# The first norm of a two-layer kernel: its weights spread over two banks by matmul, its high and low parts taken from the turned bank, the first token tile fed through alone, and identity matmuls between

## The chip, the cores and the metric

The kernel runs on one core of a Trainium2 chip. The metric is the device time of one execution in microseconds (us), as the median of several runs. The engines are TensorE (PE; its weight loads are listed as PEld), VectorE (DVE), ScalarE (ACT), GpSimd (POOL), and SyncE (SP), which issues most DMAs. A q behind an engine's name is its queue of DMA issues.

## The reference, cut to what matters

Two transformer-like layers run one after the other on 512 tokens of width 1024, in f32. The change touches only the first lines of the first layer:

```python
def rmsnorm(x, g):
    xf = x.astype(jnp.float32)
    y = xf * lax.rsqrt(jnp.mean(xf * xf, axis=-1, keepdims=True) + EPS)
    return (y * g.astype(jnp.float32)).astype(x.dtype)
...
        u = rmsnorm(h, norm_mix_pre)
        proj = u @ w_in
```

`proj` is then cut into the inputs of a short convolution and of a sparse attention; an output product, a cross attention over a memory, and a gated feed-forward stage follow. The second layer has its own norms, an mLSTM, a neighbourhood attention, a memory attention and a feed-forward stage. Every large product is a product with a weight matrix of 1024 or more rows.

## The kernel before

**Tiling.** The 512 tokens are four token tiles of 128 (`ST` = 4), each with 1024 features: `h[:, j, :]`. A product needs features on the partitions, so each normed token tile is turned: eight transposes of 128x128, four into each of two PSUM banks (`TB`, banks 4 and 5), whose result goes to `xT_high` and `xT_low`. Each f32 number is split into a high part, rounded to the format that TensorE takes at one column a beat (`fp32r`), and a low part, the rest. A product is then three matmuls: high by high, low by high and high by low. Weights are split in the same way: a chunk of 128x2048 lands in `raw`, ACT casts it to `w_high` (line 950, in `high`), and POOL subtracts to get `w_low` (line 805, in `low_parts`), in four pieces of 512.

**Order.** Each engine's program is written out by hand, and semaphores tie the engines together. `Own.link` and `Own.tell` make an engine wait for its own last instruction. The weight chunks are loaded by SP in a fixed order into three `raw` slots; a slot is loaded again when both parts of its old chunk have been made. `w_high` and `w_low` have two slots each.

**The head of the program.** For each token tile j of the first norm (phase `"x"`): ACT takes the mean square of row sums (`stat`, lines 958 and 959); DVE takes the reciprocal and multiplies the rows (`xn`, lines 1480 and 1490) into one of two `stage` buffers; PE turns them (`turn`, line 2181); DVE multiplies the turned bank by the norm weights, which lie one to a partition in `gcol`, into `qbuf` (`ql`, line 1516); ACT casts `qbuf` to `xT_high` (`hi`, line 973); DVE subtracts to `xT_low` (`ql`, line 1523). Phases in `DIRECT` have no step through `qbuf`: ACT casts straight from the turned bank (line 970), and DVE subtracts from the bank too (`lows`, line 1499).

The weights `norm_mix_pre` get into `gcol` by a load of 8 rows of 128 into `rows_in`, a transpose into bank 7 (line 2342) and a DVE copy (line 1539). The other vectors come the same way later (`vectors`, line 2348).

PE's own order is: the turned weights, token tiles 0 and 1 turned, the first chunk's product for token features of tile 0, tile 2 turned, product 1, tile 3 turned, product 2, the small vectors, product 3, then four products with the second chunk. A product here is 4 pairs of matmuls with `w_high` (lines 2291 and 2292) and 4 with `w_low` (line 2295), each 128x512. `SB` are banks 6 and 7, `ident` is the 128x128 identity, `ones` a 128x128 tile of ones, both written by POOL at the start. POOL's order at the start is its constants, `w_low` of chunks 0 and 1, then 32 one-column memsets of `invf` (line 812), which the rotary angles need.

## Time and profile before

| | us |
|---|---|
| median of 3 runs | 1724.48 (1724.47 to 1725.52) |
| the profiled execution's own time | 1727.71 |
| its span in the profile | 1726.0 |
| PE busy | 1662.4 (96%) |
| POOL / ACT / DVE busy | 729.8 / 663.8 / 621.0 |

The span runs from the first to the last instruction of the profiled execution, which took 1.7 us more than its span and 3.2 us more than the median of the runs. PE is busy nearly all the time. The mean granted clock is 0.987 of the full 2.4 GHz.

### The profile page before, as it was taken

To read this page: it belongs to the slowest core of one execution; us is meant where nothing else is said; L and a number is where in the kernel's file an instruction comes from. 1 tells how busy PE (TensorE), PEld (TensorE's weight loads), DVE (VectorE), ACT (ScalarE), POOL (GpSimd) and SP (SyncE) were. 2 spreads that over 40 slices of the span, in tenths; PEclk is the share of its full clock that TensorE was granted. 3 is DMA by queue.
4 is the path that set the end of the run, shared out by engine and by line. 5 is a ranking of instruction groups with operands and counts; after the bars stand their busy time and mean duration, and the time that the engine had idled before them with its cause. 6 is when DMAs were issued, how large, how long until landed. Compare 5 with 4: busy or idle time off the path is not lost. (4 is left out here: it accounts for less than half of the span.)

```text
span 1726.0 us, 22688 instructions
## 1 busy us (share of the span) xinstructions
PE 1662.4 (96%) x8699; PEld 1326.5 (77%) x8699; DVE 621.0 (36%) x1165; ACT 663.8 (38%) x1009; POOL 729.8 (42%) x639
## 2 busy tenths in 40 slices
PE   7989889999899999999988999999999999999999
PEld 5767667777678888878877787767788888888887
DVE  6432765442333101101137544454555331212131
ACT  5223567453343233222234534343554441313140
POOL 5223324462143444453434544323354354544443
PEclk9999999999999999999999999999999999999999
DMA  5243201332032332343221334222254323232321
GB/s 176 76 147 82 74 26 51 123 131 90 25 98 74 122 98 73 98 146 98 86 87 51 98 100 147 78 74 84 74 202 152 98 80 100 90 98 98 98 98 49
DMA packets 153020, 166.07 MB, mean 96 GB/s; under 512 B 11997, under 2 KB 114512, under 8 KB 152912
## 3 DMA queue, kind: packets, MB, share of 16 engines
q1 hardware_dynamic: 145296, 151.22, 27.7%
q10 hardware_dynamic: 7616, 13.41, 2.2%
q8 instruction: 69, 1.13, 0.3%
q14 instruction: 39, 0.32, 0.1%
HBM read 155.69 MB, written 9.30 MB: 96 GB/s over the span
## 5 line engine op out<-in xcount | busy, mean ns | idle before, releaser
L805 POOL TENSOR_TENSOR w_low<-raw,w_high 128x512 fp32r<-128x512 f32 x501 | 662.0, 1352 | 877.0 <-ACT w_high L950 876.6
L950 ACT CAST w_high<-raw 128x2048 fp32r<-128x2048 f32 x127 | 239.3, 1884 | 244.1 <-PE bank L2295 230.7
L2300 PE MATMUL bank<-xT_high,w_high 128*128 128x512 f32 (+1 forms) x672 | 249.7, 377 | 0.0
L2301 PE MATMUL bank<-xT_low,w_high 128*128 128x512 f32 (+1 forms) x672 | 248.9, 375 | 0.0
L2291 PE MATMUL bank<-w_high,hid_high 128*128 128x512 f32 x432 | 171.9, 398 | 0.0
L2292 PE MATMUL bank<-w_high,hid_low 128*128 128x512 f32 x432 | 171.7, 398 | 0.0
L2304 PE MATMUL bank<-xT_high,w_low 128*128 128x512 f32 (+1 forms) x672 | 156.7, 375 | 1.8 <-POOL w_low L805 1.7
L2205 PE MATMUL bank<-xT_high,w_high 128*128 128x512 f32 (+1 forms) x360 | 152.3, 423 | 0.7 <-ACT qbuf L1317 0.4
L2300 PEld LDWEIGHTS bank<-xT_high,w_high 128*128 128x128 f32 x672 | 127.8, 190 | 22.4
L2301 PEld LDWEIGHTS bank<-xT_low,w_high 128*128 128x128 f32 x672 | 127.7, 190 | 22.4
L2207 PE MATMUL bank<-xT_high,w_low 128*128 128x512 f32 (+1 forms) x360 | 142.4, 396 | 0.0
L2206 PE MATMUL bank<-xT_low,w_high 128*128 128x512 f32 (+1 forms) x360 | 142.0, 394 | 0.0
L2304 PEld LDWEIGHTS bank<-xT_high,w_low 128*128 128x128 f32 x672 | 120.6, 188 | 24.9 <-POOL w_low L805 2.6
L2295 PE MATMUL bank<-w_low,hid_high 128*128 128x512 f32 x432 | 119.6, 397 | 0.0
L2291 PE MATMUL bank<-w_high,xT_high 128*128 128x512 f32 x256 | 102.6, 401 | 3.3 <-DVE xT_low L1523 3.2
L2292 PE MATMUL bank<-w_high,xT_low 128*128 128x512 f32 x256 | 100.8, 394 | 0.0
L2295 PEld LDWEIGHTS bank<-w_low,hid_high 128*128 128x128 f32 x432 | 81.7, 189 | 20.0 <-POOL w_low L805 0.2
L2291 PEld LDWEIGHTS bank<-w_high,hid_high 128*128 128x128 f32 x432 | 81.7, 189 | 19.8
L2292 PEld LDWEIGHTS bank<-w_high,hid_low 128*128 128x128 f32 x432 | 81.7, 189 | 19.8
L2157 DVE TENSOR_TENSOR h<-h,bank 128x512 f32<-128x512 f32 x40 | 27.5, 688 | 173.6 <-PE bank L2295 173.5
L2205 PEld LDWEIGHTS bank<-xT_high,w_high 128*128 128x128 f32 (+1 forms) x360 | 67.8, 188 | 24.5 <-issue 9.0
L1861 DVE TENSOR_TENSOR qbuf<-silu,bank 128x512 f32<-128x512 f32 x22 | 15.1, 688 | 187.7 <-PE bank L2304 187.7
(427 smaller groups left out, 2533.1 us busy)
## 6 DMA issues: line engine op xcount, KB each, us to landing
raw<-in_w_in SPq DMA_DIRECT2D x33, 1024.0 KB, 5.2
raw<-in_w_down SPq DMA_DIRECT2D x26, 1024.0 KB, 5.0
raw<-in_w_gate_up SPq DMA_DIRECT2D x44, 512.0 KB, 5.0
raw<-in_w_up SPq DMA_DIRECT2D x16, 1024.0 KB, 5.3
raw<-in_w_kv_x SPq DMA_DIRECT2D x8, 1024.0 KB, 5.3
raw<-in_w_out SPq DMA_DIRECT2D x8, 1024.0 KB, 5.1
gate_dram<-qbuf ACTq DMA_DIRECT2D x20, 256.0 KB, 2.0
sg<-gate_dram ACTq DMA_DIRECT2D x6, 768.0 KB, 5.4
```

The costliest lines, as they stand in the source:

```text
L805: ins = pool.tensor_tensor(low[:, cs], full[:, cs], high[:, cs], ALU.subtract)
L950: own.tell(act.copy(split_slot(c, wh), split_slot(c, raw)), wh_done)
L2157: own.tell(dve.tensor_tensor(y, y, src[:, :], ALU.add), dense_v)
L2205: pe.matmul(ps, ah, bh, start=first, stop=False)
L2206: pe.matmul(ps, ah, bl, start=False, stop=False)
L2207: return pe.matmul(ps, al, bh, start=False, stop=last)
L2291: pe.matmul(ps[:, :], xh[:, k, js], ch[:, q, :], start=first and q == 0, stop=False)
L2292: pe.matmul(ps[:, :], xl[:, k, js], ch[:, q, :], start=False, stop=False)
L2295: mm = pe.matmul(ps[:, :], xh[:, k, js], cl[:, q, :], start=False, stop=last and q == len(ks) - 1)
L2300: pe.matmul(ps[:, t0:t1], ch[:, k, cs], xh[:, k, t0:t1], start=q == 0, stop=False)
L2301: pe.matmul(ps[:, t0:t1], ch[:, k, cs], xl[:, k, t0:t1], start=False, stop=False)
L2304: mm = pe.matmul(ps[:, t0:t1], cl[:, k, cs], xh[:, k, t0:t1], start=False, stop=q == len(ks) - 1)
```

## The change

1. The norm weights come as one row of 1024 (`mix_row`, on one partition), and two matmuls with a row of ones copy them onto all 128 partitions, one half into bank 6 and one into bank 7.
2. For phase `"x"`, `xn` is now two `scalar_tensor_tensor` of 128x512: rows by reciprocal by the weights in the bank. `"x"` joins `DIRECT`: highs and lows come from the turned bank, with no `qbuf`.
3. The order on ACT, DVE and PE lets token tile 0 through alone: its highs before tile 1's statistics, its lows before tile 1's `xn`, its product before tile 1 is turned. Tile 1 is turned in the middle of product 0, between its matmuls with `w_high` and those with `w_low`. ACT's cast of the second chunk (`high(1)`) moves behind the statistics of tile 3.
4. PE gets 15 matmuls of `ident` by `ident` into bank 3, whose result nobody reads: 2 ahead of the spreading, 5 behind it, 8 behind the turning of tile 0.
5. POOL writes `ones` ahead of `ident`, and the 32 memsets of `invf` ahead of `w_low`; chunk 1's `w_low` comes after `zT` and `pc`.
6. The column table loses five vectors (40 of 100 rows), of which four were loaded by SP and not read from it; SP issues four DMAs less.

```diff
--- before.py
+++ after.py
@@ -43,8 +43,7 @@
 ATT_ORDER = (0, 3, 1, 2)
 
 
-VECS = [("norm_mix_pre", 8), ("norm_x_pre", 8), ("norm_mem", 8), ("norm_ffn_pre", 8), ("g_mix_2", 8),
-        ("g_mem_2", 8), ("g_ffn_2", 8), ("norm_conv_out", 4), ("norm_attn_out", 4),
+VECS = [("norm_mem", 8), ("g_mem_2", 8), ("norm_conv_out", 4), ("norm_attn_out", 4),
         ("conv_w", 12), ("conv_w_2", 20), ("conv_b_2", 4)]
 COL = {}
 _n = 0
@@ -58,7 +57,7 @@
 GAIN_LOADS = sum(P // d for _, d in HEAD_GAINS)
 HOMES = {"gu0": 0, "if": 0, "up0": 1, "vx": 2}
 NATURAL = ("hx", "hf", "h2", "h4")
-DIRECT = NATURAL + ("hm", "hna")
+DIRECT = NATURAL + ("x", "hm", "hna")
 
 
 class Chunk:
@@ -255,11 +254,11 @@
 
     out, base, scaled = [], 0, 0
     for phase, ntok, banks, kt0, gain in (
-            ("x", ST, 2, 0, COL["norm_mix_pre"]), ("mem", MT, 2, 0, COL["norm_mem"]),
-            ("att", ST, 1, 4, COL["norm_attn_out"]), ("hx", ST, 2, 0, COL["norm_x_pre"]),
-            ("hf", ST, 2, 0, COL["norm_ffn_pre"]), ("mem2", MT, 2, 0, COL["g_mem_2"]),
-            ("h2", ST, 2, 0, COL["g_mix_2"]), ("hm", ST, 1, 0, None),
-            ("hna", ST, 1, 4, None), ("h4", ST, 2, 0, COL["g_ffn_2"])):
+            ("x", ST, 2, 0, None), ("mem", MT, 2, 0, COL["norm_mem"]),
+            ("att", ST, 1, 4, COL["norm_attn_out"]), ("hx", ST, 2, 0, None),
+            ("hf", ST, 2, 0, None), ("mem2", MT, 2, 0, COL["g_mem_2"]),
+            ("h2", ST, 2, 0, None), ("hm", ST, 1, 0, None),
+            ("hna", ST, 1, 4, None), ("h4", ST, 2, 0, None)):
         for j in ATT_ORDER if phase == "att" else range(ntok):
             out.append((phase, j, banks, base, kt0, gain, scaled))
             base += banks
@@ -364,6 +363,7 @@
         posi = at("posi", o + 13728, [P, 5], I32)
         invf = at("invf", o + 13760, [P, 32])
         ang = at("ang", 24640, [P, 5, 32])
+        mix_row = at("mix_row", 53312, [1, D])
         angk = at("angk", 25280, [P, 5, 32])
         rows_in = at("rows_in", 25920, [NCOL, P])
         pe_in = at("pe_in", 26560, [CMP, 2, 2, HD])
@@ -601,7 +601,7 @@
                 sp.dma_start(h[:, j, :], xv[:, j, :]).then_inc(x_in[j], 16)
 
             def vector_loads():
-                for name, n in VECS[1:]:
+                for name, n in VECS:
                     src = a[name]
                     src = src.rearrange("(r q) -> r q", q=P) if len(src.shape) == 1 else \
                         src.rearrange("k (r q) -> (k r) q", q=P)
@@ -766,10 +766,10 @@
             own.link(pool.memset(posi[:, :], 0))
             own.link(pool.memset(small[:, :], 0.0))
             own.tell(pool.memset(eps_col[:, :], EPS), const_ready)
+            own.link(pool.memset(ones[:, :], 1.0))
             own.link(pool.memset(ident[:, :], 0.0))
             own.tell(pool.affine_select(out=ident[:, :], in_=ident[:, :], compare_op=ALU.not_equal, fill=1.0,
                                         base=0, pattern=[[-1, P]], channel_multiplier=1), const_ready)
-            own.link(pool.memset(ones[:, :], 1.0))
             own.link(pool.memset(causal[:, :], 0.0))
             own.link(pool.affine_select(out=causal[:, 384:512], in_=causal[:, 384:512], compare_op=ALU.is_ge,
                                         fill=NEG, base=0, pattern=[[-1, P]], channel_multiplier=1))
@@ -807,9 +807,9 @@
                             own.mark(ins, wl_done)
                     own.tell(ins, wl_done)
 
-            low_parts(1)
             for j in range(32):
                 own.link(pool.memset(invf[:, j:j + 1], float(np.float32(THETA ** (-j / 32.0)))))
+            low_parts(0)
             own.link(pool.memset(zT[:, :, 0:2], 0.0))
             own.tell(pool.memset(pc[:, :, :, :], 0.0), const_ready)
             low_parts(G["gates"].chunks[-1].n)
@@ -981,15 +981,6 @@
                 dst, src = parts[-1]
                 own.tell(act.copy(dst, src), hi_done)
 
...
             def evac(group, write, between=None):
 
                 g = G[group]
@@ -1003,7 +994,7 @@
                         between(c)
 
 
-            act.dma_start(rows_in[0:8, :], a["norm_mix_pre"].rearrange("(r q) -> r q", q=P)).then_inc(mix_in, 16)
+            act.dma_start(mix_row[:, :], a["norm_mix_pre"].rearrange("(o d) -> o d", o=1)).then_inc(mix_in, 16)
             for i, n in enumerate(("pe_kc", "pe_vc")):
                 for g in range(2):
                     act.dma_start(pe_in[:, i, g, :], a[n]).then_inc(rows_in_s, 16)
@@ -1011,12 +1002,12 @@
             own.link(act.activation(rms[:, 63:64], eps_col[:, 0:1], ACT.Sqrt))
             stat(("x", 0), h[:, 0, :], D)
             high(0)
+            hi(ntile["x", 0])
             stat(("x", 1), h[:, 1, :], D)
-            hi(ntile["x", 0])
             stat(("x", 2), h[:, 2, :], D)
-            high(1)
             hi(ntile["x", 1])
             stat(("x", 3), h[:, 3, :], D)
+            high(1)
             hi(ntile["x", 2])
             hi(ntile["x", 3])
 
@@ -1480,6 +1471,14 @@
                 own.link(dve.reciprocal(rms[:, k:k + 1], rms[:, k:k + 1]))
                 if i >= 2:
                     dve.wait_ge(tr_done, NT[i - 2][3] + NT[i - 2][2])
+                if phase == "x":
+                    dve.wait_ge(vec_tr, 1)
+                    for b in range(2):
+                        cs = slice(S * b, S * b + S)
+                        ins = dve.scalar_tensor_tensor(out=stage[:, i % 2, cs], in0=h[:, j, cs], scalar=rms[:, k:k + 1],
+                                                       in1=SB[b][:, :], op0=ALU.mult, op1=ALU.mult)
+                        own.tell(ins, xn_ready) if b else own.link(ins)
+                    return
                 if phase in NATURAL:
                     dve.wait_ge(gnat_in, 16 * (NATURAL.index(phase) + 1))
                     own.tell(dve.scalar_tensor_tensor(out=stage[:, i % 2, :], in0=h[:, j, :], scalar=rms[:, k:k + 1],
@@ -1522,25 +1521,22 @@
                     q = qbuf[:, r % 2, 0:n * P].rearrange("p (k t) -> p k t", k=n)
                     own.tell(dve.tensor_tensor(dst, q, top.bitcast(F32), ALU.subtract), lo_done)
 
-            def norm(phase, ntok, width):
-                for j in range(ntok):
-                    xn(phase, j, width)
-                    if j:
-                        ql(phase, j - 1)
-                ql(phase, ntok - 1)
-
             def tile_in(name, t):
                 n = G[name].tiles[t]
                 dve.wait_ge(dense_done, n + 1)
                 return tile_bank(n)
 
 
-            dve.wait_ge(vec_tr, 1)
-            own.link(dve.tensor_copy(gcol[:, 0:8], SB[1][:, 0:8]))
-
-            norm("x", ST, D)
+            xn("x", 0, D)
+            lows("x", 0)
+            xn("x", 1, D)
+            xn("x", 2, D)
+            lows("x", 1)
+            xn("x", 3, D)
+            lows("x", 2)
+            lows("x", 3)
             dve.wait_ge(vec_tr, 2)
-            own.link(dve.tensor_copy(gcol[:, 8:NCOL], SB[0][:, 8:NCOL]))
+            own.link(dve.tensor_copy(gcol[:, 0:NCOL], SB[0][:, 0:NCOL]))
             own.link(dve.tensor_copy(peT[:, :, :], SB[0][:, P:P + 2 * CMP].rearrange("p (i c) -> p i c", i=2)))
 
             dve.wait_ge(const_ready, 4)
@@ -2255,7 +2251,7 @@
                     low_seen[0] = need
                     pe.wait_ge(wl_done, need)
 
-            def product(c, k_tile, xh, xl, ntok=S, piece=None, part=None):
+            def product(c, k_tile, xh, xl, ntok=S, piece=None, part=None, between=None):
 
                 if True:
                     g = c.group
@@ -2290,6 +2286,8 @@
                             for q, k in enumerate(ks):
                                 pe.matmul(ps[:, :], xh[:, k, js], ch[:, q, :], start=first and q == 0, stop=False)
                                 pe.matmul(ps[:, :], xl[:, k, js], ch[:, q, :], start=False, stop=False)
+                            if between:
+                                between()
                             for q, k in enumerate(ks):
                                 low_ready(c, q)
                                 mm = pe.matmul(ps[:, :], xh[:, k, js], cl[:, q, :], start=False,
@@ -2337,14 +2335,22 @@
                 turned_ready(phase, ST if phase not in ("mem", "mem2") else MT)
 
 
+            def keep_warm(n):
+                for _ in range(n):
+                    pe.matmul(bank[3][:, 0:P], ident[:, :], ident[:, :], start=True, stop=True)
+
             pe.wait_ge(const_ready, 2)
+            keep_warm(2)
             pe.wait_ge(mix_in, 16)
-            pe.transpose(SB[1][:, 0:8], rows_in[0:8, :], ident[0:8, 0:8]).then_inc(vec_tr, 1)
+            for b in range(2):
+                mm = pe.matmul(SB[b][:, :], ones[0:1, :], mix_row[:, S * b:S * b + S], start=True, stop=True)
+            mm.then_inc(vec_tr, 1)
+            keep_warm(5)
             turn("x", 0)
-            turn("x", 1)
+            keep_warm(8)
 
             def vectors():
-                pe.wait_ge(rows_in_s, 16 * (len(VECS) - 1 + 2 * GROUPS))
+                pe.wait_ge(rows_in_s, 16 * (len(VECS) + 2 * GROUPS))
                 pe.transpose(SB[0][:, 0:NCOL], rows_in[:, :], ident[0:NCOL, 0:NCOL])
                 for i in range(2):
                     mm = pe.transpose(SB[0][:, P + CMP * i:P + CMP * (i + 1)], pe_in[:, i, :, :].rearrange(
@@ -2353,7 +2359,7 @@
             q_first, q_last = G["q"].chunks
             for j in range(ST):
                 turned_ready("x", j + 1)
-                product(q_first, j, xTh, xTl)
+                product(q_first, j, xTh, xTl, between=(lambda: turn("x", 1)) if j == 0 else None)
                 if j < 2:
                     turn("x", j + 2)
                 if j == 2:
```

On PE, from its first matmul to the end of product 0, the kernel before has (`stage` are the normed rows, `rows_in` the 8 rows of norm weights):

```order
L2342 MATMUL bank<-ident,rows_in 128x8
L2181 MATMUL bank<-ident,stage 128x128 x16
L2291 MATMUL bank<-w_high,xT_high 128x512
L2292 MATMUL bank<-w_high,xT_low 128x512
...
L2291 MATMUL bank<-w_high,xT_high 128x512
L2292 MATMUL bank<-w_high,xT_low 128x512
L2295 MATMUL bank<-w_low,xT_high 128x512 x4
```

and with the change, over the same place:

```order
L2340 MATMUL bank<-ident 128x128 x2
L2346 MATMUL bank<-mix_row,ones 128x512 x2
L2340 MATMUL bank<-ident 128x128 x5
L2177 MATMUL bank<-ident,stage 128x128 x8
L2340 MATMUL bank<-ident 128x128 x8
L2287 MATMUL bank<-w_high,xT_high 128x512
...
L2288 MATMUL bank<-w_high,xT_low 128x512
L2177 MATMUL bank<-ident,stage 128x128 x8
L2293 MATMUL bank<-w_low,xT_high 128x512 x4
L2177 MATMUL bank<-ident,stage 128x128 x8
L2287 MATMUL bank<-w_high,xT_high 128x512
```

The second half of the 16 transposes has moved from ahead of product 0 to inside it.

On ACT, from the cast of the first weight chunk to the last highs of the norm, the kernel before has:

```order
L950 CAST w_high<-raw 128x2048
L958 ACTIVATE junk,rms<-h 128x1024
L959 ACTIVATE rms<-rms,eps_col 128x1
L973 CAST xT_high<-qbuf 128x4x128 x2
L958 ACTIVATE junk,rms<-h 128x1024
L959 ACTIVATE rms<-rms,eps_col 128x1
L950 CAST w_high<-raw 128x2048
L973 CAST xT_high<-qbuf 128x4x128 x2
L958 ACTIVATE junk,rms<-h 128x1024
L959 ACTIVATE rms<-rms,eps_col 128x1
L973 CAST xT_high<-qbuf 128x4x128 x4
```

and with the change:

```order
L950 CAST w_high<-raw 128x2048
L970 CAST xT_high<-bank 128x4x128 x2
L958 ACTIVATE junk,rms<-h 128x1024
L959 ACTIVATE rms<-rms,eps_col 128x1
L958 ACTIVATE junk,rms<-h 128x1024
L959 ACTIVATE rms<-rms,eps_col 128x1
L970 CAST xT_high<-bank 128x4x128 x2
L958 ACTIVATE junk,rms<-h 128x1024
L959 ACTIVATE rms<-rms,eps_col 128x1
L950 CAST w_high<-raw 128x2048
L970 CAST xT_high<-bank 128x4x128 x4
```

Tile 0's highs moved ahead of tile 1's statistics, and the second cast of weights moved back by one tile's statistics and one tile's highs.

On DVE, over the first two token tiles, the kernel before has:

```order
L1480 RECIPROCAL rms<-rms 128x1
L1490 TENSOR_SCALAR stage<-h,rms 128x1024
L1480 RECIPROCAL rms<-rms 128x1
L1490 TENSOR_SCALAR stage<-h,rms 128x1024
L1516 TENSOR_TENSOR qbuf<-bank,gcol 128x512 x2
L1523 TENSOR_TENSOR xT_low<-qbuf,xT_high 128x4x128 x2
```

and with the change:

```order
L1471 RECIPROCAL rms<-rms 128x1
L1478 SCALAR_TENSOR_TENSOR stage<-h,rms,bank 128x512 x2
L1498 TENSOR_TENSOR xT_low<-bank,xT_high 128x4x128 x2
L1471 RECIPROCAL rms<-rms 128x1
L1478 SCALAR_TENSOR_TENSOR stage<-h,rms,bank 128x512 x2
L1471 RECIPROCAL rms<-rms 128x1
L1478 SCALAR_TENSOR_TENSOR stage<-h,rms,bank 128x512 x2
L1498 TENSOR_TENSOR xT_low<-bank,xT_high 128x4x128 x2
```

Tile 0's lows no longer stand behind tile 1's rows, and the two multiplications into `qbuf` are gone.

## Rows read from the trace of the kernel before

**Rows 1.** The page: busy time of PE, and the chain that ended last by engine.

```profile
PE 1662.4 (96%) x8699; PEld 1326.5 (77%) x8699; DVE 621.0 (36%) x1165; ACT 663.8 (38%) x1009; POOL 729.8 (42%) x639
...
PE 32%; DVE 0%; issue 0%; ACT 0%; DVEq 0%; ACTq 0%
```

**Rows 2.** Timeline of PE: start, length in us, instruction, [idle before, its releaser].

```profile
2.92 0.24 PE L2342 MATMUL bank<-ident,rows_in 8*128 8x8 f32 x1 [2.92 <-DMA rows_in<-in_norm_mix_pre]
7.51 1.97 PE L2181 MATMUL bank<-ident,stage 128*128 128x128 f32 x8 [4.35 <-DVE stage L1490]
...
15.94 0.79 PE L2291 MATMUL bank<-w_high,xT_high 128*128 128x512 f32 x1 [0.88 <-DVE xT_low L1523]
...
21.23 1.26 PE L2181 MATMUL bank<-ident,stage 128*128 128x128 f32 x8
22.24 0.48 PE L2291 MATMUL bank<-w_high,xT_high 128*128 128x512 f32 x1
...
25.08 1.04 PE L2181 MATMUL bank<-ident,stage 128*128 128x128 f32 x8
...
32.39 0.39 PE L2291 MATMUL bank<-w_high,xT_high 128*128 128x512 f32 x1
```

**Rows 3.** Timeline of ACT, same columns.

```profile
4.92 1.06 ACT L958 ACTIVATE junk<-h 128x1024 bf16<-128x1024 f32 x1
...
6.10 0.30 ACT L959 ACTIVATE rms<-rms,eps_col 128x1 f32<-128x1 f32 x1
7.17 1.90 ACT L950 CAST w_high<-raw 128x2048 fp32r<-128x2048 f32 x1 [0.77 <-DMA raw<-in_w_in]
...
34.82 1.91 ACT L950 CAST w_high<-raw 128x2048 fp32r<-128x2048 f32 x1
```

**Rows 4.** Timeline of DVE, same columns.

```profile
6.50 0.16 DVE L1480 RECIPROCAL rms<-rms 128x1 f32<-128x1 f32 x1 [3.14 <-ACT rms L959]
6.70 0.75 DVE L1490 TENSOR_SCALAR stage<-h,rms 128x1024 f32<-128x1024 f32 x1
...
12.28 1.42 DVE L1516 TENSOR_TENSOR qbuf<-bank,gcol 128x512 f32<-128x512 f32 x2
13.79 2.10 DVE L1523 TENSOR_TENSOR xT_low<-qbuf,xT_high 128x512 fp32r<-128x512 f32 x2
```

**Rows 5.** Timeline of POOL, same columns.

```profile
4.58 0.14 POOL L783 MEMSET rpb_zero<- 1x64 f32 x1
9.22 5.39 POOL L805 TENSOR_TENSOR w_low<-raw,w_high 128x512 fp32r<-128x512 f32 x4 [4.50 <-ACT w_high L950]
17.99 6.36 POOL L805 TENSOR_TENSOR w_low<-raw,w_high 128x512 fp32r<-128x512 f32 x4 [3.38 <-ACT w_high L950]
24.41 4.94 POOL L812 MEMSET invf<- 128x1 f32 x32
```

**Rows 6.** Groups by form: line, engine, operation, shapes, count | busy us, mean ns | idle before.

```profile
L2053 DVE SCALAR_TENSOR_TENSOR decay<-bank,decay 128x512 f32<-128x512 f32 x8 | 5.5, 692 | 10.4 <-PE bank L2659 10.3
L1499 DVE TENSOR_TENSOR xT_low<-bank,xT_high 128x512 fp32r<-128x512 f32 x32 | 22.1, 692 | 15.5 <-ACT xT_high L970 14.5
L970 ACT CAST xT_high<-bank 128x512 fp32r<-128x512 f32 x32 | 18.8, 587 | 21.4 <-PE bank L2181 20.8
```

**Rows 7.** Timeline around a later norm whose highs come from the bank.

```profile
359.73 1.03 PE L2181 MATMUL bank<-ident,stage 128*128 128x128 f32 x8
360.42 1.20 ACT L970 CAST xT_high<-bank 128x512 fp32r<-128x512 f32 x2 [0.66 <-PE bank L2181]
```

**Rows 8.** Timeline of PE where plain f32 columns run at the full clock.

```profile
228.80 1.12 PE L2493 MATMUL bank<-conv_scale,ones 128*128 128x512 f32 x2 [0.74 <-DVE conv_scale L1671]
229.86 1.13 PE L2450 MATMUL bank<-kT,qT 64*128 64x512 f32 x4
```

**Rows 9.** Timeline of PE around a later rise of the clock.

```profile
109.32 0.79 PE L2205 MATMUL bank<-xT_high,w_high 128*128 128x512 f32 x1
...
114.03 0.40 PE L2207 MATMUL bank<-xT_high,w_low 128*128 128x512 f32 x1
```

More of the change, by code:

```diff
@@ L982, in hi_grid @@
                 own.tell(act.copy(dst, src), hi_done)
-            def norm(phase, ntok, width):
-                for j in range(ntok):
-                    src = SOURCES[phase]
-                    stat((phase, j), src[:, j, :], width)
-                    if j:
-                        hi(ntile[phase, j - 1])
-                hi(ntile[phase, ntok - 1])
             def evac(group, write, between=None):
@@ L1523, in ql @@
                     own.tell(dve.tensor_tensor(dst, q, top.bitcast(F32), ALU.subtract), lo_done)
-            def norm(phase, ntok, width):
-                for j in range(ntok):
-                    xn(phase, j, width)
-                    if j:
-                        ql(phase, j - 1)
-                ql(phase, ntok - 1)
             def tile_in(name, t):
```

## The prediction

> **What bounds the kernel now.** I read the page first. PE is busy 96% of the span, and the chain that ended last has PE with 32%, and 0% each for DVE, ACT and their queues [rows 1]: once its products run, PE waits for almost nobody. So what moves PE's first products moves the end by as much, provided that no stage further on was paced by something that the change leaves where it was. Hence I read the timeline of PE over the head of the program, then those of the engines it waits for.
>
> PE's first product starts at 15.94, and the first of the four products with the second chunk at 32.39 [rows 2]. From there on the order is as before. The quantity that I follow is that second start.
>
> Two things are lost before it. First, a relay: the rows of tile 0 are ready at 7.45 [rows 4] and turned from 7.51 to 9.48 [rows 2], but DVE takes them up only at 12.28, because tile 1's rows stand ahead of them; then come four steps through `qbuf`. Second, the clock. Product 0 takes 21.23 - 15.94 = 5.29 us, product 1 only 25.08 - 22.24 = 2.84 [rows 2], for the same 12 matmuls. The turning takes 1.97 us at 7.51 and 1.04 at 25.08. So PE runs at 1.2 GHz up to about 21.2 and at 2.4 GHz from there. It had worked without a pause since 15.94, so the rise came 5.3 us after steady work began. At the later rise, steady products begin at 109.32 and the short duration is there at 114.03 [rows 9]: 4.7 us.
>
> **The change, step by step.** Times are those of the profiled execution.
>
> *Weights spread.* POOL writes `ones` ahead of `ident`, which makes `ident` about 0.35 us later, at 2.4; the two first identity matmuls run in the wait for the load. The load of 8 rows of 512 bytes is there by 2.92 [rows 2]. The new one moves the same 4 KB to one partition; the trace has no such load. Bounds: 2.92, and 4.92, by when the 512 KB of tile 0 are there [rows 3]. I take 2.95. The two spreading matmuls have 512 plain f32 columns; the nearest row starts two of them 1.06 us ahead of the next group at 2.4 GHz [rows 8], so at most 2.1 us for two at 1.2 GHz. The weights are then in the banks at 5.1 (at the late bound 7.1). DVE can't use them before tile 0's reciprocal ends at 6.66 [rows 4]. So the step costs nothing at 2.95, and 0.4 us at the late bound. The gain column's copy on DVE was idle time anyway.
>
> *Five identity matmuls.* A 128-column pass cost 0.24 us at 1.2 GHz (1.97 for 8) [rows 2], so they end at 6.3; PE would be idle until 8.2. Cost nothing.
>
> *Tile 0's rows.* One `tensor_scalar` of 0.75 us [rows 4] becomes two `scalar_tensor_tensor` of 128x512 with one input in a bank. The same operation with such an input takes 0.692 [rows 6], so 6.70 + 2 x 0.73 = 8.13: 0.7 us later than before. PE turns from 8.18 to 10.15.
>
> *Highs and lows.* In the later norm, ACT starts the highs 0.69 us after the turning starts at the full clock [rows 7]; at half the clock the first four transposes take 1 us and the step about 0.2. So ACT starts at 9.35, when its cast of the first chunk is done (9.07) [rows 3]. Two highs of 0.587 and two lows of 0.692 [rows 6] interleave: highs 9.35 to 9.95 and 10.25 to 10.85, lows to 10.6 and 11.6. The eight identity matmuls fill PE from 10.15 to 12.0, and since they are in order ahead of the product they, not the lows, set its start: **product 0 starts at 12.0** instead of 15.94.
>
> *The clock.* PE now works steadily from 8.18. By the two cases above the rise comes 4.7 to 5.3 us later, at 12.9 to 13.5; I take 13.4. Eight matmuls with `w_high` from 12.0: 3.3 of them at 0.427 us, the rest at 0.23, to 14.5 (512 columns at 1.2 GHz are 0.427 us; 0.23 is a twelfth of a product at the full clock, rounded down).
>
> *Tile 1.* ACT takes its statistics only after tile 0's highs: 10.87 + 1.48 (4.92 to 6.40 for tile 0) [rows 3] = 12.35; DVE has the rows at 14.08. PE turns them from 14.5; highs to 16.4, lows at 16.55 and 17.25. Meanwhile PE does the four matmuls with `w_low`. POOL has to do 32 memsets first (4.94 us, now from 4.75 to 9.7), then four pieces of 5.39/4 = 1.35 [rows 5]: ready at 11.1, 12.4, 13.8 and 15.1, and wanted from 15.5 on. Cost nothing; with the slower pace of 6.36 for four, the last comes at 16.1, just when it is wanted.
>
> *Tiles 2 and 3.* Turning 2 needs the banks free, at 16.55 and 17.25, so product 1 runs from 17.8 to 20.55. ACT does tile 3's statistics (to 17.9) and now the second weight cast (to 19.8) ahead of tile 2's highs: these come at 19.8 and 20.45, lows at 21.2 and 21.9. PE waits for them 0.7 us and once more 0.2; product 2 from 22.45 to 25.2, small vectors 0.4, product 3 from 25.6 to **28.35**, where it was 32.39. The gain at this point is **4.0 us**.
>
> *Behind it.* `w_low` of the second chunk is made from 19.85 to at most 26.2 (6.36) [rows 5] and wanted at 30.2. The rotary angles hang on the small vectors, which come 4 us sooner; the third chunk's cast, at 34.82 [rows 3], waits for the sine behind them and moves along. The four loads that SP no longer issues were behind the data that PE waits for; worth nothing. With no other engine in the chain [rows 1] I let all 4.0 us through. The profile gives 1726.0 - 4.0; the profiled run took 1727.71, 3.2 more than the median, so the sum goes to the median: 1724.48 - 4.0 = **1720.5**.
>
> A bound on each side. If the rise comes before 12.0, the products with `w_high` end at 13.8, but tile 1's rows are there only at 14.08, so the gain is at most 4.4 (1720.1). If it comes at 15.0, they end at 15.25 and all behind is 0.75 later: gain 3.3 (1721.2).
>
> **What a rule would make of it.** The group of two plain f32 matmuls of 512 columns and the group behind it start 1.06 us apart [rows 8], 0.53 each; one beat a column is 0.213, so this is two passes and a start. The Trainium skill (FP8 and Floating Point Precision, TensorE Precision Notes) says that true FP32 takes four passes through the array. By it the eight identity matmuls at 1.2 GHz would take 3.4 us instead of 1.9, which is its own case below; the trace disagrees with it.
>
> **The rivals.**
> - *The identity matmuls don't bring the clock up.* They multiply mostly zeros, and the turning at 7.51 was not followed by a rise before 21.2. Then steady work counts from 12.0, and the rise comes near 17: product 0 with `w_high` to 15.4, turning 1 to 17.4, lows of tile 1 at 18.45, product 1 from 19.0, product 2 from 23.7, second chunk at 29.5. Gain 2.85: 1721.6. Nothing in the trace decides; chance 0.17.
> - *Identity matmuls twice as long* (four passes): product 0 starts at 13.6, gain about 2.5: 1722.0. Against it stands the row on plain f32; chance 0.03.
> - *Something further on holds its time*, so that the later stages give part of the 4 us back. For it: PE has 1726.0 - 1662.4 = 63.6 us of idle time in all [rows 1], of which not 12 lie ahead of product 0. Against it: those waits are on ACT, DVE and POOL, which themselves wait for PE. Half given back: 1722.5; chance 0.07.
> - *Slower: the row of weights comes late.* It is one run of 4 KB where there were eight of 512 bytes, and may queue behind the row tiles and weight chunks that are loaded at the same time. Each us by which the banks are ready after 6.66 moves tile 0's rows. If the load comes with the first weight chunk, at 7.17 [rows 3], the banks are ready at 9.3 and the gain is 1.4 (1723.1): chance 0.04. From a landing at 8.6 on, the change is slower; behind the fourth row tile and the second chunk, at about 12, it would be 1727.9: chance 0.04. Against both: the 8-row load was through in 2 us under the same traffic.
> - *More than counted*: the later stretches at half the clock fall differently on the work, and the run is nearer 1718.5. They can fall worse as well, which is in the forecast's own range. Chance 0.07.
>
> **The numbers.** The forecast has 0.58. 0.2% of this time is 3.4 us, about what a measurement of this kernel can tell from no change, so the border lies at 1721.0. The forecast's own range is 1719.6 to 1721.6, mostly below the border: four fifths of 0.58 are faster, with the last rival 0.54; the rest of the forecast and the cases at 1721.6 to 1723.1 make 0.41 "within"; slower 0.05. The range that leaves out the slower case and the outer part of the last rival is 1718.4 to 1723.2.
>
> **What would show each step.** In the profile after: the spreading matmuls by 3 and the banks ready by 5.2; tile 0's rows at 8.1; the first product at about 12.0, its matmuls turning from 0.43 to 0.23 us apart at 12.9 to 13.5; tile 1 turned at 14.5; the second chunk's first product at about 28.35 and the third cast near 30.7. The prediction is wrong if the first product starts after 12.5 (late weights or long identity matmuls), if the pace rises after 15, or if the second chunk starts at 28.4 and the end has moved less: then a later stage holds its own time.

## The result, and the profile after

| | before | after |
|---|---|---|
| median of 4 runs each, same chip, us | 1725.0 (1724.47 to 1729.08) | 1711.77 (1705.77 to 1716.15) |
| profiled execution, us | 1727.71 | 1716.15 |
| its span, us | 1726.0 | 1714.4 |
| mean granted clock | 0.987 | 0.985 |

The ratio of the times is 0.9922 [0.9905, 0.9940]: 13.2 us less, where I had forecast 4.0, and outside the range. The page of the kernel after has PE as busy as before; 33 more PE records, and less busy time than in [rows 1]:

```profile
PE 1660.4 (97%) x8732; PEld 1330.9 (78%) x8732; DVE 616.3 (36%) x1160; ACT 663.6 (39%) x1009; POOL 728.8 (43%) x639
...
PE 32%; DVE 0%; issue 0%; ACT 0%; DVEq 0%; ACTq 0%
```

The timeline of PE over the head, which answers to [rows 2]:

```profile
2.40 1.22 PE L2340 MATMUL bank<-ident 128*128 128x128 f32 x4 [2.40 <-POOL ident L771]
3.55 3.78 PE L2346 MATMUL bank<-mix_row,ones 1*128 1x512 f32 x4
7.25 2.50 PE L2340 MATMUL bank<-ident 128*128 128x128 f32 x10
9.55 1.92 PE L2177 MATMUL bank<-ident,stage 128*128 128x128 f32 x8
11.26 2.88 PE L2340 MATMUL bank<-ident 128*128 128x128 f32 x16
13.89 0.48 PE L2287 MATMUL bank<-w_high,xT_high 128*128 128x512 f32 x1
...
15.82 1.04 PE L2177 MATMUL bank<-ident,stage 128*128 128x128 f32 x8
16.61 1.17 PE L2293 MATMUL bank<-w_low,xT_high 128*128 128x512 f32 x4
18.12 1.29 PE L2177 MATMUL bank<-ident,stage 128*128 128x128 f32 x8 [0.34 <-DVE xT_low L1498]
...
29.98 0.39 PE L2287 MATMUL bank<-w_high,xT_high 128*128 128x512 f32 x1
```

Two things stand in it. The counts: two identity matmuls in the code are four records here, five are ten, eight are sixteen, and the two spreading matmuls are four. A plain f32 matmul thus shows as two records, a transpose of f32 as one (x8 for eight). And the second chunk's product starts at 29.98, where it was 32.39: the head has given 2.4 us, not 4.0. The timelines of DVE and ACT, against [rows 4] and [rows 3], show the first delay, the rows of tile 0 waiting for the weights in the bank:

```profile
7.45 1.53 DVE L1478 SCALAR_TENSOR_TENSOR stage<-h,rms,bank 128x512 f32<-128x512 f32 x2 [0.78 <-PE bank L2346]
11.39 0.69 DVE L1498 TENSOR_TENSOR xT_low<-bank,xT_high 128x512 fp32r<-128x512 f32 x1 [2.41 <-ACT xT_high L970]
```

```profile
10.70 0.58 ACT L970 CAST xT_high<-bank 128x512 fp32r<-128x512 f32 x1 [1.52 <-PE bank L2177]
...
32.37 1.91 ACT L950 CAST w_high<-raw 128x2048 fp32r<-128x2048 f32 x1
```

The span is 11.6 us shorter, so more than 9 us come from behind 30 us, where the code of the engines is as before. I set each PE instruction of after against the same one of before. How much earlier it starts:

| at (us) | 100 | 300 | 500 | 700 | 900 | 1240 | 1400 | 1500 | 1600 | end |
|---|---|---|---|---|---|---|---|---|---|---|
| earlier by (us) | 2.4 | 5.1 | 5.7 | 6.8 | 8.2 | 6.8 | 7.4 | 8.4 | 9.7 | 11.5 |

(The steps back, of 1.4 us between 900 and 1240 and of 1.5 us behind 1240, are two stretches of 3.4 us at half the clock that only after has.) Of the 2.7 us between 100 and 300, 1.6 are the products behind 137.65, which ran at half the clock in before and at the full clock in after, and 0.9 one turning at 221.46 for the same reason; the other differences there nearly cancel. Behind 300 the lead grows in no single wait. It grows steadily while PE runs the products that read `hid`, `yT`, `hmT` or `oxT`, and stays flat in those that read `xT`. The timeline of PE in such a product, of before and then of after, both at a granted clock of 1.00; between the first and the last row of each lie five products of 12 matmuls:

```profile
630.12 1.10 PE L2295 MATMUL bank<-w_low,hid_high 128*128 128x512 f32 x4
...
632.93 1.10 PE L2295 MATMUL bank<-w_low,hid_high 128*128 128x512 f32 x4
...
644.18 1.10 PE L2295 MATMUL bank<-w_low,hid_high 128*128 128x512 f32 x4
```

```profile
632.14 1.08 PE L2293 MATMUL bank<-w_low,hid_high 128*128 128x512 f32 x4
...
634.89 1.07 PE L2293 MATMUL bank<-w_low,hid_high 128*128 128x512 f32 x4
...
645.87 1.07 PE L2293 MATMUL bank<-w_low,hid_high 128*128 128x512 f32 x4
```

The sixty matmuls took 644.18 - 630.12 = 14.06 us before, 234 ns each, and 645.87 - 632.14 = 13.73 us after, 229 ns each. The same instructions with the same operands run 2% faster. There are 1296 such matmuls on `hid` (at 5.4 ns that makes 7.0 us), 192 each on `yT` and `hmT`, 192 on `oxT`.

What differs is where the operands lie. `hid`, `yT`, `hmT`, `oxT` and `memT` are views into one block, `arena` (`at(...)`). It is allocated behind `gcol`, the column table, which shrank by 40 of its 100 f32 a partition: the arena starts at byte 147776 of a partition after, and at 147936 before. Modulo 256 that is 64 after and 224 before. `xT`, `w_high` and `w_low` lie ahead of it and begin at 128 modulo 256 in both.

### The profile page after: what moved, and what is told of

Its sections match the earlier page's. It is cut to its first block and busy times, and to the rows that moved or that the text cites. A ratio compares the mean times of both kernels' runs of the same rounds, so it can differ in the third digit from the quotient of the medians.

```text
span 1714.4 us, 22737 instructions
## 1 busy us (share of the span) xinstructions
PE 1660.4 (97%) x8732; PEld 1330.9 (78%) x8732; DVE 616.3 (36%) x1160; ACT 663.6 (39%) x1009; POOL 728.8 (43%) x639
## 5 line engine op out<-in xcount | busy, mean ns | idle before, releaser
L2288 PEld LDWEIGHTS bank<-w_high,hid_low 128*128 128x128 f32 x432 | 81.6, 189 | 17.2
```

The costliest lines, as they stand in the source:

```text
L2288: pe.matmul(ps[:, :], xl[:, k, js], ch[:, q, :], start=False, stop=False)
```

## The experiments

Theory P (placement): the 9 us come from the position of the arena alone. Rival H (head): they are a late result of the earlier start, of loads or of clock stretches. The second question is what the identity matmuls, the spreading and the new order each do in the head.

All runs in one table. The change is the median less that of the kernel before on the same chip (1725.2 for e1 to e4, 1724.2 for e5 to e8, 1725.18 for e9 to e12). "2nd chunk" is the start of its first product in the profiled execution. "Pace" is worked out from the trace: for each pair of operands, the mean time from one PE start to the next of the 512-column matmuls at the full clock, times their number, summed over all pairs; before has 1248.2 us.

| run | change, us | ratio | 2nd chunk | pace, us |
|---|---|---|---|---|
| before | | | 32.39 | 1248.2 |
| after | -13.2 | 0.9922 [0.9905, 0.9940] | 29.98 | 1238.8 |
| e1_pad32 | -5.3 | 0.9972 [0.9962, 0.9981] | 32.66 | 1245.1 |
| e2_pad96 | -9.3 | 0.9943 [0.9929, 0.9956] | 32.50 | 1238.8 |
| e3_after_pad32 | -4.8 | 0.9969 [0.9956, 0.9981] | 29.57 | 1246.8 |
| e4_no_ident | -13.8 | 0.9919 [0.9906, 0.9933] | 29.09 | 1238.8 |
| e5_hid64 | -7.2 | 0.9955 [0.9938, 0.9972] | 32.38 | 1240.3 |
| e6_noid_pad64 | -11.9 | 0.9929 [0.9915, 0.9944] | 30.11 | 1237.6 |
| e7_noid_pad128 | -3.8 | 0.9978 [0.9969, 0.9986] | 29.75 | 1246.3 |
| e8_old_order | -13.2 | 0.9922 [0.9907, 0.9938] | 29.42 | 1238.6 |
| e9_front64 | -13.2 | 0.9920 [0.9907, 0.9933] | 30.08 | 1238.7 |
| e10_all_at_128 | -16.1 | 0.9904 [0.9891, 0.9916] | 29.93 | 1235.1 |
| e11_ident_turned | -16.4 | 0.9900 [0.9887, 0.9914] | 28.77 | 1238.9 |
| e12_order_only | +2.4 | 1.0011 [1.0002, 1.0020] | 33.70 | 1248.5 |

### Placement without the change: e1, e2

The kernel before, with an unused tensor right ahead of the arena, in e1 of 8 f32 a partition (arena at 0 modulo 256), in e2 of 24 (at 64, as in after):

```diff
+        sb("pad", [P, 8])       # e1; e2: sb("pad", [P, 24])
         arena_bytes = 77888
```

> The kernel before with one unused tile of 32 bytes a partition ahead of the arena, so that everything in the arena (hid, yT, hmT, oxT, memT) lies 32 bytes further on, at a multiple of 64 bytes; nothing else is changed. Theory A, the place of the arena: 512-column matmuls that stream from the arena were 234 ns apart before and 229 with the change, those that stream xT, ahead of the arena, 227 in both; here they fall to about 229, some 1900 matmuls by 5 ns, so 9 us less than before: about 1716. Theory B, the time behind the head is won by the head's order (other half-clock stretches, other meetings of engines): no change, 1725, and the pace stays 234.

> The kernel before with an unused tile of 96 bytes, so that the arena's start is 64 more than a multiple of 128, as it is in the changed kernel. Theory A with steps of 64 bytes: as with 32 bytes, about 1716. Theory A with steps of 128 bytes: one of the two padded kernels gains 9 us and the other not, or less. Theory B: 1725.

With the old head whole (second chunk at 32.50), e2 is 9.3 us faster, and its pace is that of after to 0.1 us. Theory P holds, and rival H falls: an unused tensor brings what the change brought behind the head. e1, at another position, has a third of it in its pace (3.1 us) and is 5.3 us faster, between the 9 us and the nothing that I had expected of the two theories. (The expectations speak of matmuls that stream from the arena. In the products of 512 columns only `hmT` is the moving operand, the one that is streamed; `hid`, `yT` and `oxT` are the stationary one.)

### The change with the gain taken away: e3, e7

The kernel after with 8 f32 ahead of the arena (at 96), and, without identity matmuls, with 32 f32 (at 192):

```diff
+        sb("pad", [P, 8])       # e3; e7: sb("pad", [P, 32]), and no keep_warm
         arena_bytes = 77888
```

> The changed kernel with an unused tile of 32 bytes ahead of the arena, so that the arena starts 32 more than a multiple of 64, as in the kernel before. Theory A: the pace in the arena is 234 ns again, and only the head's 2.4 us are left: about 1722.5. Theory B: as the changed kernel, 1712.

> As the last, with 128 bytes ahead of the arena: again 64 more than a multiple of 128. If steps of 128 bytes decide, as without the tile: pace 229, 1711.4.

Both keep the early head and lose most of the rest: -4.8 and -3.8 us. That is the order of what the head alone is worth. For e7 I had expected the pace of after, if steps of 128 bytes decide; they don't.

### Which position, and relative to what: e5, e6, e9, e10

e5 is e1 with the two `hid` tensors alone put at 64; e6 is e4 with the arena at 128; e9 is e4 with 16 f32 ahead of `h`, which moves every tensor behind it, weights and arena alike, by 64 bytes; e10 is e4 with the `hid`, `hmT` and `oxT` highs shifted by 64 within the arena, so that they and their lows lie at 128.

```diff
-        hidh, hidl = at("hid_high", 0, [P, 8, S], F32R), at("hid_low", 16384, [P, 8, S], F32R)
+        hidh, hidl = at("hid_high", 64, [P, 8, S], F32R), at("hid_low", 16448, [P, 8, S], F32R)   # e5, e10
+        sb("pad", [P, 16])      # e6, ahead of the arena
+        sb("front", [P, 16])    # e9, ahead of h
```

> The kernel before with the 32-byte tile (arena at a multiple of 128 bytes), and of the arena's tensors only hid_high and hid_low moved another 64 bytes, into a gap behind them. Theory A, the pace hangs on the bytes at which the operand itself lies: in the down projections the 232.6 ns of the 32-byte kernel become about 229, as at 64 more than a multiple of 128, some 1290 matmuls by 3.5 ns, so 4.5 us less than with the 32-byte tile (1719.9 there), about 1715.5, and the hmT and yT matmuls keep that kernel's pace. Rival C, it is the arena as a whole (its other tensors, which ScalarE, VectorE and GpSimd read and write meanwhile): the pace stays 232.6 and the time 1720.

> The changed kernel without identity matmuls (1711.4), with 64 bytes ahead of the arena: a multiple of 128, and the same bytes modulo 256 as the tensors ahead of the arena, which are streamed at 227. If being at the same place modulo 256 as those is what counts, the pace falls to 227 and the time to about 1709. If it is as with the 32-byte tile on the kernel before, also at a multiple of 128 but not at the same place modulo 256, the pace is 232.5 and the time 1715.

> The changed kernel without identity matmuls, with an unused tile of 64 bytes ahead of the very first tile, h: every tensor lies 64 bytes further on, and none moves against another. If it is the distance between the two operands of a matmul that counts (modulo 256 the arena lies 64 under the weights), nothing changes: 1711.4, xT 227 and hid 229. If it is each operand's own place modulo 256, with 128 the best: the arena is now at 128 and hid goes to 227, but xT and the weights go to 192, where hid had 231 to 236: some 3600 matmuls by 4 to 8 ns, 15 to 28 us slower: 1726 to 1740.

> The changed kernel without identity matmuls, with hid_high and hid_low, hmT_high and oxT_high moved 64 bytes within the arena, so that they too lie at 128 modulo 256, as yT, hmT_low and oxT_low already do. By the table of paces so far: hid from 229.1 to 227, some 1290 matmuls by 2.1 ns, and a little for the others: 3 us less than 1711.4, so 1708.4. If the tensors' other users count, no change.

The mean ns from start to start, worked out from the traces. The first of a pair is the moving operand, the second the stationary one:

| pair | before | after | e1 | e3 | e5 | e6 | e7 | e9 | e10 |
|---|---|---|---|---|---|---|---|---|---|
| arena begins at, mod 256 | 224 | 64 | 0 | 96 | 0 | 128 | 192 | 128 | 64 |
| w_high, hid_high | 234.4 | 229.2 | 232.7 | 232.3 | 229.1 | 226.9 | 235.7 | 229.1 | 226.9 |
| w_high, hid_low | 234.3 | 229.5 | 232.4 | 234.5 | 229.6 | 226.8 | 231.2 | 229.6 | 226.7 |
| w_low, hid_high | 234.2 | 228.4 | 232.6 | 233.4 | 228.4 | 227.0 | 233.4 | 228.4 | 226.9 |
| w_high, yT_low | 233.2 | 226.9 | 228.6 | 234.7 | 228.5 | 235.7 | 232.0 | 227.0 | 226.8 |
| hmT_high, w_high | 234.3 | 227.4 | 237.2 | 232.4 | 237.6 | 233.2 | 231.2 | 227.3 | 226.9 |
| xT_low, w_high | 227.5 | 227.5 | 227.6 | 227.5 | 227.4 | 227.6 | 227.6 | 227.5 | 227.6 |

In e5 only `hid` moved, and its pace fell from 232.7 to 229.1 against e1, while the other rows stayed within 0.4 ns, so it is not the arena as a whole. In e9 the arena begins at 128, as in e6, but the weights moved with it, to 192, and every row reads as after: what counts is the distance between the two operands modulo 256, not the address. At distance 0 the pace is 227 ns (`hid` in e6 and e10, `yT_low` in after, at 64 + 49216, which is 128 modulo 256); with the operand 64 bytes below the weights (`hid` in after and e5, `yT_low` in e1) it is 228 to 230 ns; at the other distances tried, 231 to 238. The modulus is 256: with all the weights in the same place, the arena of e2 (at 148032) lies 256 bytes behind that of after, so they differ modulo 512, and the two paces are the same; that of e7 lies 128 bytes behind, and its paces are slow. e10 has nearly all pairs at distance 0 and the shortest pace, 1235.1. `hmT_high` in e6 stands at distance 0 and is slow, 233.2, where `hmT_low`, the next matmul's operand, stands at +64; in e10 both stand at 0, and it is 226.9. So the time to the next start seems to hang on what the next matmul reads as well; this one case is all that there is for it. For this reason e6 missed its forecast of 1709: `hid` reached 227, but `yT_low` and `hmT` became slower, and the time is 1712.28. The timeline of PE in e10, as above; five products between the first and the last row:

```profile
631.13 1.07 PE L2293 MATMUL bank<-w_low,hid_high 128*128 128x512 f32 x4
...
644.73 1.08 PE L2293 MATMUL bank<-w_low,hid_high 128*128 128x512 f32 x4
```

13.60 us for sixty, 226.7 ns each. e10's ratio is below that of after (0.9904 against 0.9922), but the intervals overlap, as they do with e9, which has the same head and ran on the same chip: there e10 is 2.9 us faster, where the paces give 3.6. Which part of the chip makes the distance matter no run shows.

### The head: e4, e8, e11, e12

e4 is the kernel after without its identity matmuls:

```diff
-            keep_warm(2)
...
-            keep_warm(5)
...
-            keep_warm(8)
```

> The changed kernel without its 15 identity matmuls. Theory A doesn't speak of them: the arena's pace stays 229, and only the head changes. The spread starts at 2.95 and ends near 6.5, tile 0 is turned from 8.2, product 0 starts at 11.7 instead of 13.9, but at half the clock to about 17; the second chunk's first product at 29.5 to 30.5 against 29.98, so the total is that of the changed kernel within 1 us. If the identity matmuls matter by what they do to the clock, it is 1.5 us or more slower.

Its time is that of after (1711.37 against 1711.77). The timeline of its PE:

```profile
2.40 3.78 PE L2345 MATMUL bank<-mix_row,ones 1*128 1x512 f32 x4 [2.40 <-POOL ident L771]
8.12 1.97 PE L2177 MATMUL bank<-ident,stage 128*128 128x128 f32 x8 [1.94 <-DVE stage L1478]
11.62 0.80 PE L2287 MATMUL bank<-w_high,xT_high 128*128 128x512 f32 x1 [1.53 <-DVE xT_low L1498]
...
14.66 0.40 PE L2288 MATMUL bank<-w_high,xT_low 128*128 128x512 f32 x1
14.89 1.04 PE L2177 MATMUL bank<-ident,stage 128*128 128x128 f32 x8
```

Product 0 starts 2.3 us before that of after, but at half the clock: 0.43 us from start to start up to 14.34, then 0.23. The identity matmuls do bring the rise forward, to about 13.2 in after and 10.6 in e3 (its sixteen records from 10.97 on take 1.95 us, against 2.88), from 14.4 here; and in the four others without them (e6, e7, e9, e10) the turning of tile 1, at 15.23 to 15.28, takes 1.33 to 1.91 us, so the rise there falls inside it (15.9 in e7, 16.5 in e10) or just behind it (about 17 in e6 and e9). But as made they hold PE until 13.89, or 12.87 in e3. The two cancel: the second chunk starts at 29.98 and 29.57 with them, and at 29.09 to 30.11, mean 29.8, in the five kernels without.

e11 keeps them but makes each a transpose, one record in place of two:

```diff
-                    pe.matmul(bank[3][:, 0:P], ident[:, :], ident[:, :], start=True, stop=True)
+                    pe.transpose(bank[3][:, 0:P], ident[:, :], ident[:, :])
```

> The changed kernel with its 15 identity matmuls issued as transposes, which the trace shows as one instruction of one pair where a plain f32 matmul shows as two. If the term that I mis-sized is their length: each takes 0.21 at half the clock instead of 0.42, the eight end at about 11.6 to 12.3 and product 0 starts at 12.0 to 12.4 instead of 13.89; the second chunk's first product comes at 28.4 to 29.2 instead of 29.98, the total about 1 us below the changed kernel's. If the clock then rises later, the gain is smaller.

The timeline of its PE:

```profile
6.73 1.33 PE L2340 MATMUL bank<-ident 128*128 128x128 f32 x5
8.50 1.94 PE L2177 MATMUL bank<-ident,stage 128*128 128x128 f32 x8 [0.44 <-DVE stage L1478]
10.26 1.05 PE L2340 MATMUL bank<-ident 128*128 128x128 f32 x8
11.97 0.50 PE L2287 MATMUL bank<-w_high,xT_high 128*128 128x512 f32 x1 [0.66 <-DVE xT_low L1498]
...
14.52 1.09 PE L2177 MATMUL bank<-ident,stage 128*128 128x128 f32 x8 [0.44 <-DVE stage L1478]
```

The clock is up from 10.3 on (eight in 1.05 us, where the eight turnings before them took 1.94), product 0 starts at 11.97 at the full pace, and tile 1 is turned at 14.52. The second chunk starts at 28.77, the earliest of all. The run is 16.4 us faster than before, 3.2 us faster than e9 on the same chip, of which the head explains 1.3.

e8 is e4 with the order of before on all engines (item 3 of the change and `w_low` ahead of POOL's constants undone); e12 is the kernel before with nothing but the new order, still through `qbuf`:

```diff
+            turn("x", 1)                                                  # e8, PE
...
-                product(q_first, j, xTh, xTl, between=(lambda: turn("x", 1)) if j == 0 else None)
+                product(q_first, j, xTh, xTl)
...
-            norm("x", ST, D)                                              # e12, DVE
+            xn("x", 0, D)
+            ql("x", 0)
+            xn("x", 1, D)
+            xn("x", 2, D)
+            ql("x", 1)
```

> The changed kernel without identity matmuls and with the old order on all engines: two token tiles turned ahead of product 0, tile 1's statistics and rows ahead of tile 0's highs and lows, the second weight cast back in its place, low parts ahead of the 32 memsets. What is left of the head's change is the spread and the highs and lows from the bank. If the order makes the head's gain: product 0 starts near 14.9 and the second chunk near 31.4, about 2.3 us later than without identity matmuls (29.09), total about 1713.7. If the spread and the missing step through qbuf make it, the total stays within 1 us of 1711.4.

> The kernel before with the new order alone on all engines (token tile 0 first, tile 1 turned inside product 0, the second weight cast and the low parts at their new places); weights still by transpose and qbuf, no spread, no identity matmuls, arena where it was (224 modulo 256). If the order is as good by itself as the spread was: product 0 starts near 12 and the second chunk near 29.5 to 30.5 instead of 32.39, 2 to 3 us less: 1721.5 to 1722.5. If not, the rest of the chain through qbuf takes it back: the second chunk above 31.5 and no change beyond 1 us.

In e8 the second chunk starts at 29.42, among those with the new order, and the time is e4's (1711.03 and 1711.37). In e12 the product of tile 0 starts early, at 12.67, but the head ends 1.3 us later than before. The timelines of PE and of DVE in e12:

```profile
19.70 0.50 PE L2298 MATMUL bank<-w_high,xT_high 128*128 128x512 f32 x1 [0.85 <-DVE xT_low L1523]
...
26.00 0.79 PE L2298 MATMUL bank<-w_high,xT_high 128*128 128x512 f32 x1 [2.40 <-DVE xT_low L1523]
26.60 0.63 PE L2299 MATMUL bank<-w_high,xT_low 128*128 128x512 f32 x1
27.02 0.63 PE L2298 MATMUL bank<-w_high,xT_high 128*128 128x512 f32 x1
...
29.50 1.09 PE L2304 MATMUL bank<-w_low,xT_high 128*128 128x512 f32 x4
```

```profile
12.85 1.46 DVE L1490 TENSOR_SCALAR stage<-h,rms 128x1024 f32<-128x1024 f32 x1
...
20.66 0.75 DVE L1490 TENSOR_SCALAR stage<-h,rms 128x1024 f32<-128x1024 f32 x1
21.45 1.42 DVE L1516 TENSOR_TENSOR qbuf<-bank,gcol 128x512 f32<-128x512 f32 x2
23.06 2.89 DVE L1523 TENSOR_TENSOR xT_low<-qbuf,xT_high 128x512 fp32r<-128x512 f32 x2 [0.19 <-ACT xT_high L973]
```

Behind the wait of 2.40 us the granted clock is 0.50 from 26.0 to 29.4, the only such stretch that a head has behind its first rise: the eight matmuls with `w_high` of product 2 take 3.50 us, where those of product 1 took 1.95 (19.70 to 21.65). These 1.55 us are more than the 1.3 that the head lost; without them it would have ended some 0.3 us earlier than before, an estimate from these rows. Whether the other runs of e12 have this stretch too is not known.

Behind the waits stands DVE. The same DVE instructions have two lengths. The multiplication of the rows takes 0.75 us while POOL rests and 1.46 while POOL makes `w_low`; the subtraction from `qbuf` takes 1.45 a piece (2.89 for two) beside `w_low`. In after, where it reads the bank, two take 1.42 both at 17.28, with POOL idle, and at 21.88, beside `w_low`; and POOL's `w_low` takes 4.97 and 5.03 us there, where [rows 5] have 5.39 and 6.36. The timelines of DVE and of POOL in after:

```profile
17.28 1.42 DVE L1498 TENSOR_TENSOR xT_low<-bank,xT_high 128x512 fp32r<-128x512 f32 x2
...
21.88 1.42 DVE L1498 TENSOR_TENSOR xT_low<-bank,xT_high 128x512 fp32r<-128x512 f32 x2 [0.83 <-ACT xT_high L970]
```

```profile
9.79 4.97 POOL L805 TENSOR_TENSOR w_low<-raw,w_high 128x512 fp32r<-128x512 f32 x4
...
21.31 5.03 POOL L805 TENSOR_TENSOR w_low<-raw,w_high 128x512 fp32r<-128x512 f32 x4 [5.79 <-ACT w_high L950]
```

The Trainium skill (GPSIMD Engine Reference, Specifications) says that GpSimd shares its SBUF interfaces with VectorE, and that instructions of DVE in a 2-port mode or with two SBUF inputs contend with it. The trace agrees for the subtraction, which has two such inputs from `qbuf` and one from the bank; in which mode the multiplication runs it doesn't show.

So of the head's parts it is the spread weights and the way past `qbuf` that pay, under either order; no run has one of the two without the other. The new order without them ends the head later, by way of a wait and the clock's fall behind it, and with them brings nothing that shows.

### Do the parts add up?

For each profiled execution I set three terms against its span, all as differences to the profiled kernel before: the start of the second chunk, the pace, and half of the time between that start and PE's last matmul for which the granted clock was at half (44.4 us in before, between 30.7 and 51.2 in the others).

| run | head | pace | half clock / 2 | sum | span |
|---|---|---|---|---|---|
| after | -2.4 | -9.4 | +3.4 | -8.4 | -11.6 |
| e1_pad32 | +0.3 | -3.1 | 0.0 | -2.8 | -5.0 |
| e2_pad96 | +0.1 | -9.4 | -1.7 | -11.0 | -11.8 |
| e3_after_pad32 | -2.8 | -1.4 | -1.7 | -5.9 | -10.9 |
| e4_no_ident | -3.3 | -9.4 | -3.4 | -16.1 | -17.2 |
| e5_hid64 | 0.0 | -7.9 | +3.4 | -4.5 | -6.4 |
| e6_noid_pad64 | -2.3 | -10.6 | 0.0 | -12.9 | -14.2 |
| e7_noid_pad128 | -2.6 | -1.9 | -1.7 | -6.2 | -7.1 |
| e8_old_order | -3.0 | -9.6 | -6.8 | -19.4 | -21.7 |
| e9_front64 | -2.3 | -9.5 | -1.7 | -13.5 | -14.8 |
| e10_all_at_128 | -2.5 | -13.1 | -3.4 | -19.0 | -19.9 |
| e11_ident_turned | -3.6 | -9.3 | -3.4 | -16.3 | -16.9 |
| e12_order_only | +1.3 | +0.3 | 0.0 | +1.6 | +0.4 |

Every span is shorter than its sum would have it, by 0.6 to 3.2 us and in e3 by 5.0, so something that the three terms leave out ran against the profiled kernel before. Part of it is found. PE's waits around its sums of `stage` and the product with `conv_scale` behind them, at about 221 us, come to 3.1 us in before (2.39 of them an idle stretch for which the profile names no releaser, and 0.74 on `conv_scale`) and to about as much in the others, but to 1.5 in e3 and e8. That closes most of e8's gap; 3.4 us of e3's stay unexplained. Its median, at -4.8, is near the sum of its head and pace (-4.2). The stretches at half the clock scatter from one execution to the next, by up to 20 us of half clock or 10 us of time, in no relation to the edits that I can see, and may carry much of what the medians leave open.

## Why the prediction was wrong

**The missing term, 9.4 us.** The step that failed is that of the column table: in the change I listed that it "loses five vectors (40 of 100 rows)", and in "Behind it" I costed only its loads ("worth nothing"). I never asked what lies behind the table in SBUF. The arena moved by 160 bytes, from a distance of 96 to one of -64 bytes against the weights modulo 256. No rival held it: "something further on" and "more than counted" were the nearest, and the second had 0.07 and 2 us. "From there on the order is as before" was true and not enough, since the pace was not. e2 shows the term alone: 9.3 us with the old head.

**Plain f32 matmuls, twice as long.** I read "x2" in [rows 8] as two matmuls in 1.06 us, hence 0.53 each and two passes. It was one matmul with two records. At half the clock the two spreading matmuls take 7.25 - 3.55 = 3.70 us, 1.85 each, which is four passes of 0.427 and a little; the 1.06 at the full clock is four of 0.213 and a little. So they end at 7.3, not at 5.1; tile 0's rows are ready at 8.98, not at 8.13 (a sum which should read 8.16); the five identity matmuls, which I had put at no cost, hold PE until 9.55, where the turning was to start at 8.18 and does start at 8.12 in e4; the eight take 2.6 us (11.26 to 13.89) though the clock rose in them; and product 0 starts at 13.89, not at 12.0. Of these 1.9 us, 1.1 lie ahead of the eight and 0.8 in them. This was the rival "identity matmuls twice as long", which I gave 0.03: it put product 0 at 13.6 and the gain at 2.5; the trace has 13.89 and 2.4. The Trainium skill (FP8 and Floating Point Precision, TensorE Precision Notes) gives true FP32 four passes, and I wrote that the trace disagrees; the trace agrees, and my count was wrong. In e11, with half the records, product 0 starts at 11.97, where I had put it, but for another reason: the clock is up from 10.3, the eight are done by 11.3, and product 0 waits 0.66 us for tile 0's lows.

**The clock, right by luck.** The rise forecast for 12.9 to 13.5 came at 13.2 in after, but the reasoning that gave it failed. I had counted 4.7 to 5.3 us of steady work from 8.18. In after PE had no pause from 2.40 on, so the rise came 10.8 us after steady work began; in e3, which has none from 2.40 on either, it came at 10.6, after 8.2 us; in e11 at 10.3, 1.8 us behind the last pause; in e4 at 14.4, 2.8 us behind it. The rival that the identity matmuls don't bring the clock up falls: in the three kernels with them the rise came at 10.3 to 13.2, in the five without them and with the same order at 14.4 to 17. What I had not weighed is that they cost PE as much as the rise gives.

**Tile 1 and behind.** Tile 1 was turned at 15.82, not 14.5, for product 0 came later; `w_low` was never waited for in the head, as forecast. The waits on the lows ahead of turnings 2 and 3 came as 0.34 and 0.56 us, where I had about 0.9 before product 2. The head's 2.4 us were let through, as the lead shows, which is still 2.4 us at 100.

**The late row of weights** did not happen: the spreading begins as soon as `ident` is there (2.40 in e4), so the row was there too.

## What to carry to other kernels

When an edit changes the size of any tensor, list what is allocated behind it, and read the start-to-start time of matmuls on those tensors before and after: here an unused pad of 96 bytes was worth 9.3 us of 1725, more than the whole rewrite of the head. Before taking a duration from a row, count how many records one instruction of that kind leaves. A matmul that only keeps the clock up should be of the shortest kind, and must not stand ahead of ready work.

The kernel that the runs point to is e10's placement with e11's transposes; it was not run. Of those run, e10 (1709.1) and e11 (1708.83) are the fastest, and they can't be told apart.

## What the runs showed of the hardware that I had not expected

- A 512-column matmul on split f32 operands has a pace of 226.7 to 237.6 ns at the same granted clock, and the distance between its two operands in the partition, modulo 256 bytes, decides most of it: 227 at 0, 228 to 230 at -64, 231 to 238 at the others tried, with `hmT_high` out of line where its neighbour stood elsewhere (233.2 at 0 in e6, 227.4 at -64 in after). The cause in the chip stays open.
- Between two groups of the same matmuls PE can stand still for 2.1 to 2.7 us with nothing in the profile to release it (at about 220 us in before, e1, e5, e7 and e12); in the other kernels it doesn't. No run shows why.
- A plain f32 matmul leaves two records and takes twice as long as a transpose of the same columns: at half the clock five identity matmuls take 2.30 us (7.25 to 9.55 in after), 0.46 each, and eight transposes 1.94, 0.24 each.
- The moment of the first rise of the clock is not fixed for one program head: 14.4 to about 17 us in five kernels with the same head (e4, e6, e7, e9, e10).
- DVE's multiplication of the rows took 1.46 us beside POOL's `w_low` and 0.75 without (e12); the subtraction with an input in a bank kept 0.71 either way (after).
